# Expert down weights with two neighbouring rows per partition, and the gated rows turned with a stride of two

## The reference, cut to what matters

```python
def hier_moe(h, w_rg, b_rg, w_re, b_re, w_g, w_u, w_d):
    ...
    gates = jnp.sum(jax.nn.one_hot(ids, N_EXPERTS, dtype=jnp.float32) * wts[..., None], axis=1)
    hid = jax.nn.silu(jnp.einsum("nd,edf->nef", x, w_g)) * jnp.einsum("nd,edf->nef", x, w_u)
    y = jnp.einsum("nef,efd->nd", hid * gates[:, :, None].astype(x.dtype), w_d)
```

## Time and profile before

| | us |
|---|---|
| median of 3 runs (842.76 to 843.53) | 843.4 |
| the profiled execution's own time | 847.0 |
| its span in the trace | 845.0 |
| PE busy | 785.5 (93%) |
| DVE busy | 321.5 (38%) |
| ACT busy | 166.5 (20%) |
| moved by DMA | 291.47 MB, mean 345 GB/s |

### The profile page before, as it was taken

One profiled execution on the slowest core, in us unless ns is written; L12 is line 12 of the kernel. 1 busy time (PEld: TensorE's weight loads), 2 busy tenths in 40 slices (PEclk: granted clock), 3 DMA queues, 4 the chain that ended last, 5 costly groups with the idle time before them and its releaser, 6 DMA issues.

```text
span 845.0 us, 15981 instructions
## 1 busy us (share of the span) xinstructions
PE 785.5 (93%) x6910; PEld 524.4 (62%) x6910; DVE 321.5 (38%) x687; ACT 166.5 (20%) x323; POOL 12.3 (1%) x17
## 2 busy tenths in 40 slices
PE   3999999998999999999977989989999999998697
PEld 3788568677898655556542444679865545664244
DVE  1155467653414433433332340223353344333224
ACT  3112411323203111111100141040321111111013
POOL 0000001020000000000000000000000000000000
PEclk9999999999999999999998999999999999999798
DMA  9999779493899599999999999996549999999993
GB/s 342 387 371 386 254 261 353 147 344 104 274 390 399 222 414 363 362 417 415 420 415 411 400 387 385 389 409 243 200 147 417 384 361 417 416 419 415 413 402 144
DMA packets 97879, 291.47 MB, mean 345 GB/s; under 512 B 11833, under 2 KB 14991, under 8 KB 87567
## 3 DMA queue, kind: packets, MB, share of 16 engines
q1 hardware_dynamic: 86960, 284.32, 87.3%
q10 hardware_dynamic: 10847, 6.11, 2.5%
HBM read 288.30 MB, written 2.10 MB: 344 GB/s over the span
## 4 chain that ended last, share of the span: by engine, by line
PE 74%; SPq 11%; DMA 7%; DVE 2%; ACT 2%; issue 2%; ACTq 1%; DVEq 0%
PE psum L1360 7%; PE psum L1262 7%; PE psum L905 7%; PE psum L1335 6%; PE psum L1345 6%; PE psum L1392 5%; PE psum L858 5%; PE psum L965 5%; DMA scratch<-in_w_exp_up 5%; SPq L742 5%; PE psum L1536 4%; PE psum L1549 3%; PE psum L1403 3%; SPq L761 2%; PE psum L1027 2%
## 5 line engine op out<-in xcount | busy, mean ns | idle before, releaser
L1345 PE MATMUL psum<-scratch,hT 128*32 128x512 f32 (+1 forms) x384 | 77.0, 647 | 16.5 <-DMA ring<-in_w_exp_up 8.7
L1335 PE MATMUL psum<-scratch 128*128 128x128 f32 x704 | 82.9, 276 | 0.9 <-DVE scratch L2478 0.9
L1335 PEld LDWEIGHTS psum<-scratch 128*128 128x128 f32 x704 | 80.5, 192 | 1.3 <-issue 1.2
L1345 PE MATMUL psum<-ring,hT 128*32 128x512 f32 (+1 forms) x288 | 67.7, 619 | 5.1 <-DMA scratch<-in_w_exp_up 5.1
L905 PE MATMUL psum<-hT,ring 128*128 128x256 f32 x256 | 57.8, 383 | 1.1 <-DVE hT L2069 0.7
L1403 PEld LDWEIGHTS psum<-const,scratch 128*128 128x128 bf16 x480 | 45.1, 97 | 21.5 <-issue 13.6
L1403 PE MATMUL psum<-const,scratch 128*128 128x256 bf16 x480 | 55.9, 272 | 1.5 <-DVE scratch L2494 1.5
L1345 PEld LDWEIGHTS psum<-scratch,hT 128*32 128x32 f32 (+1 forms) x384 | 21.0, 122 | 54.1 <-issue 54.1
L905 PEld LDWEIGHTS psum<-hT,ring 128*128 128x128 f32 x256 | 47.9, 190 | 9.6 <-DVE hT L2069 2.0
L2487 DVE TENSOR_SCALAR hT<-psum,const 128x512 f32<-128x512 f32 x22 | 16.5, 751 | 95.1 <-PE psum L1392 93.6
L1903 ACT ACTIVATE scratch<-psum 128x256 f32<-128x256 f32 x22 | 8.4, 383 | 211.4 <-PE psum L1345 124.8
(11 more groups left out here) (337 smaller groups left out, 1033.0 us busy)
## 6 DMA issues: line engine op xcount, KB each, us to landing
ring<-in_w_mod SPq DMA_DIRECT2D x40, 1024.0 KB, 11.2
scratch<-in_w_exp_down SPq DMA_DIRECT2D x28, 1024.0 KB, 15.7
ring<-in_w_exp_down SPq DMA_DIRECT2D x24, 1024.0 KB, 17.5
scratch<-in_w_exp_gate SPq DMA_DIRECT2D x22, 1024.0 KB, 16.6
scratch<-in_w_exp_up SPq DMA_DIRECT2D x22, 1024.0 KB, 18.3
ring<-in_w_exp_gate SPq DMA_DIRECT2D x18, 1024.0 KB, 15.5
ring<-in_w_exp_up SPq DMA_DIRECT2D x18, 1024.0 KB, 18.6
scratch<-in_w_exp_gate SPq DMA_DIRECT2D x26, 512.0 KB, 8.0
```

The source lines that it names most:

```text
L1335: last = mm(bank[b][:, k * P:(k + 1) * P], hrow[:, t, half * 4 + k, :], Pm[:, t, :], start=(t == 0), stop=(t == 1))
L1345: last = mm(bank[0][i * m:(i + 1) * m, :], xg[:, k, i * m:(i + 1) * m], w[e][:, k, :, :], start=(k == 0), stop=(k == KT - 1))
```

## The change

The down weights are taken with rows 2p and 2p + 1 in partition p, in all three functions that load them. The two rows are neighbours in HBM and in SBUF, so `expert_down` now moves one piece of 8 KB per partition where there were two of 4 KB. In `half_down` the pieces stay at 2 KB, only the rows change. The single expert of a slot is no longer split by a (128 partitions with 4 KB each, twice) but by partitions: first the partitions 0 to 63, then 64 to 127 (`HB` is 64), with 8 KB each. To match, `turn` transposes the even columns of `hid` for a = 0 and the odd ones for a = 1, read with a stride of two, instead of the first and the second 128.

```diff
             def half_down(l, c, ids, half):
-                wd = I["w_exp_down"][l].rearrange("e (a p) n -> e p a n", a=2)
+                wd = I["w_exp_down"][l].rearrange("e (p a) n -> e p a n", a=2)
...
             def expert_down(l, c, ids):
-                wd = I["w_exp_down"][l].rearrange("e (a p) n -> e p a n", a=2)
+                wd = I["w_exp_down"][l].rearrange("e (p a) n -> e p a n", a=2)
...
                     if len(ids) == 2:
                         sp.dma_start(dst, wd[e]).then_inc(full[s], 16)
                     else:
-                        for a in range(2):
-                            sp.dma_start(dst[:, a], wd[e][:, a]).then_inc(full[s], 16)
+                        for r in (slice(0, HB), slice(HB, P)):
+                            sp.dma_start(dst[r], wd[e][r]).then_inc(full[s], 16)
...
             def turn(sem):
                 for a in range(2):
-                    nc.tensor.transpose(bank[0][:, a * P:(a + 1) * P], hid[:, a * P:(a + 1) * P], ident)
+                    nc.tensor.transpose(bank[0][:, a * P:(a + 1) * P], hid.rearrange("p (n a) -> p a n", a=2)[:, a, :], ident)
```

## The result

The changed kernel takes 863.9 us, median of 5 runs (860.9 to 866.9), against 843.5 us before (842.8 to 844.3). The ratio is 1.0225, with a 95% interval of 1.0194 to 1.0256: 19 us slower by the ratio, 20.3 us by the medians. 850.5 was predicted, with 855.5 as the upper end.

A forecast was written before the change was run, and what follows sets the result against it. The prediction took the full DMA queue late in both expert stages as the bound. Its terms, -2.6 + 9.7 + 0 + 0 = +7.1 us on 843.4, gave 850.5 us, range 840.4 to 855.5.

The forecast's parts named there:

- What bounds the kernel: Late expert stages, both layers: the full DMA queue bounds; its changes reach the end nearly one for one.
- Part 1: Whole down loads, line 761: 8 KB pieces gain 0.065 us for each of 20 experts a layer, 2.6 us in both.
- Part 2: Split down loads, line 764: 64 partitions load at half rate, +2.43 us for each of four experts, +9.7 us.
- Part 3: half_down, line 751: pieces stay 2 KB in the same number, behind the last gate and up loads; zero.
- Part 4: The turn's strided transposes: taken as zero; doubling would add 0.22 us per turn, at most 1.8 us in all.
- Does the cost reach the end?: Last half of pass 10: PE's wait grows to 2.9 and 3.1 us, whole delay kept, no clock loss taken.
- rival 4: Half rate, plus longer waits lowering PE's clock (3.0 us) and strided turns costing double (1.8 us): 855.3 us; chance 0.10.
- Rival 1: Line 764's 64-partition loads run at full rate; all 22 experts a layer gain 0.065 us: 840.5 us; chance 0.19.
- Rival 2: Engines out of step hide half of the split loads' loss, +1.2 us per split expert: 845.7 us; chance 0.12.
- Rival 3: Larger pieces in the down loads gain nothing and the halves cost nothing: 843.4 us; chance 0.09.

The follow-up runs named there:

- the version with no one-sided load: The changed kernel with line 764 alone put back to two loads over all 128 partitions, 4 KB pieces each: 843.2 us, ratio 0.9985.
- the long run: Eight halves following one another in the changed kernel with every whole down load (line 761) split by partitions too; that kernel took 984.8 us, single run.
- the split alone: The kernel before with only line 764 changed to partitions 0 to 63, then 64 to 127, two 4 KB pieces per partition: 867.3 us, ratio 1.0285.

## Why the prediction was wrong

**What bounds the kernel** was read rightly. The loss of the queue reached the end, also that of the mono some 100 us ahead of it, as the run with only the mono's expert split shows. Whether the queue would swallow something at 343 or 684 no run tests: all four holes lie behind these points.

**Part 1**, the larger pieces: -2.6 us predicted. The rate is there (422 GB/s in the window 398:418, and packets as computed), and the five runs without a one-sided load show -1.3, -1.1, -2.4, -1.7 and -3.4 us (the last for partitions 32 to 95), with intervals of about 2 us to either side. All five have the sign, and in two of them the interval leaves out zero. Their mean, 2.0 us, is near the 2.6 to 2.9 that were expected.

**Part 2** is the step that failed, in one term: "+2.43 us, four times, +9.7 us". Which resource and which direction were right; the term's size was wrong, because the price of the ends of a run was not in it, a mechanism that no row of before showed. The term measures 20.2 us, 5.1 for an expert. It has three pieces.
- The half rate itself is 2.16 us for an expert, from the 225 GB/s of the long run. Predicted 2.43.
- The ends of a run of halves slow the whole loads around it. I took the stream as one pipe: a half load at half rate, then full rate again. In the four holes of the changed kernel (rows below) against the run with line 764 put back the loss is 24 x (1 - 339 / 415) = 4.4, 20 x (1 - 327 / 408) = 4.0, 24 x (1 - 366 / 423) = 3.2 and 24 x (1 - 326 / 408) = 4.8 us. The mean is 4.1, so the ends cost 1.9 us there, as against the 2.5 of the long run. This piece was put at nothing.
- 5.1 - 4.1 = 1.0 us for an expert is left, 4 us in all, hardly more than the 3 us to either side of the 20.2.

The four holes of the changed kernel:

```profile
365.00:389.00 24.00, 24.00 (x202) 14.18 (x204) 8.18 (x13) 4.32 (x11) 0.00 (x0) 1.00 1.01 339
451.00:471.00 20.00, 13.28 (x98) 3.61 (x97) 4.92 (x6) 1.28 (x2) 0.00 (x0) 0.83 1.02 327
...
718.00:742.00 24.00, 24.00 (x192) 12.69 (x192) 8.49 (x13) 3.70 (x8) 0.00 (x0) 1.00 1.01 366
800.00:824.00 24.00, 18.16 (x144) 9.55 (x144) 6.76 (x10) 1.73 (x5) 0.00 (x0) 0.86 1.02 326
```

Do the first two pieces alone give the other times? With 2.16 us for an expert and 2.5 us for a run of halves, the changed kernel comes out at 4 x 2.16 + 4 x 2.5 = 18.6 us above the version with no one-sided load (measured 20.2), the mono alone at 9.3 (8.4), the kernel with the whole three split at 8 x 2.16 + 4 x 2.5 = 27.3 (27.1), and all down loads split, 44 experts in 14 runs, at 130 (140). The 2.5 was read from the last of these, the other three were not used for it; they agree within their intervals of about 3 us. Only the split alone, 24 us, lies above it by more than its interval.

For what is left there is one sign in the changed kernel. Near the end of layer 0, while its last gate and up load is on its way (it lands at 494.10) and behind it, two windows of the changed kernel read as the first two lines here; the third is the same place in the kernel with the split alone, whose last product of that kind starts at 486.46:

```profile
490.00:494.00 4.00, 2.79 (x25) 2.23 (x24) 0.00 (x0) 0.00 (x0) 0.00 (x0) 1.00 0.84 300
494.00:498.00 4.00, 3.76 (x33) 1.24 (x34) 0.00 (x0) 0.07 (x1) 0.00 (x0) 1.00 0.85 239
...
482.00:486.00 4.00, 2.82 (x25) 2.25 (x24) 0.00 (x0) 0.00 (x0) 0.00 (x0) 1.00 1.04 397
```

At a DMA share of 0.84 some engines have nothing to move while others still bring the load that PE waits for. With 300 and 239 GB/s, where the split alone has 397 and then 387 (486:490), these 8 us lose about 2.5 us, and that doesn't lie in the four windows above. But the split alone has no such stretch (its share is 1.04 there), so it is no fixed part of the price. It is also one execution against another: the two whose windows are compared took 866.9 and 842.1 us, 24.8 apart and not 20.2. That a load is late because its slowest engine is late, and that engines out of step are also why a single pair of halves disturbs the loads before and after it, is an inference. No run here brings the engines into step, and no row tells them apart, so it stays open.

The Trainium skill states in SBUF — State Buffer, section "Door 1: The DMA port swizzle", that bit 6 of the partition number chooses between the two ports of a cluster, and that 0 to 31 cover the same 8 ports as 0 to 63. These runs agree on both: 32 to 95 has no loss (0.9960), the quarters of 32 lose as much as the halves (1.0216 against 1.0225). Its asymptote of 218 GB/s for eight ports stands against 225 measured in the long run. What its section "Can I just issue two DMAs to hit both halves?" says of two such loads, that they serialize, fits too; the runs show that they cost more than that.

**Part 3** was right as far as can be seen: the split alone, without the new rows in the last pass, loses as much. **Part 4** was nearer to zero than to the doubling: 0.02 us per turn in the one that was read.

**Does the cost reach the end?** The wait before the last half was to grow to 3 us. Instead both halves of the last pass wait. In layer 0 it is 2.53 and 1.45 us, since the queue was later than I had it. The clock, rival 4, did fall at the first of them, in the changed kernel's timeline and in the window behind it:

```profile
484.07 1.07 PE L1360 MATMUL psum<-ring,hT 128*32 128x512 f32 x2 [2.53 <-DMA scratch<-in_w_exp_up]
484.08 1.07 PE L1360 MATMUL psum<-scratch,hT 128*32 128x512 f32 x2
484.89 1.10 PE L1360 MATMUL psum<-ring,hT 128*32 128x512 f32 x2
...
484.00:487.00 3.00, 2.93 (x16) 0.91 (x20) 2.33 (x3) 0.00 (x0) 0.00 (x0) 0.50 1.02 399
```

Four products start 0.82 us after the four before, twice the 0.43 at full clock, for 3 us. It costs nothing there, because PE waits again for the second half, 1.45 us at 494.24.

**The rivals.** Rival 1 (full rate) fell with the split alone. Rival 2 (half of the loss hidden, because the engines are out of step) fell too: more was lost than the half rate, not less. Rival 3 (no gain, no loss) fell with the rates. Rival 4 was right in that more is lost than the half rate, but not by its means.

## What to carry to other kernels

A DMA should have partitions on both sides of partition 64: split a load by what lies within each partition, as line 764 did before, or by even and odd partitions, not into 0 to 63 and 64 to 127. In a full queue one such pair cost about twice what its own half rate says, and the price was handed on to the end through 100 us of full queue. If a semaphore's count is the only reason for a second load, the count can be changed instead: one load of 1 MiB was as fast.

## What the runs showed of the hardware that was not expected

- Two halves of an expert among whole loads cost 4.1 us of the queue's time and 5.1 us at the end, against 2.16 us for an expert within a run of halves.
- The DMA share stays at 1.00 while the rate falls to 186 GB/s. So the share alone doesn't show this loss; GB/s does.
- 64 partitions with a step of two load at full rate (420 GB/s in the window with both loads), and so do partitions 32 to 95 (421 GB/s).
- A transpose of float32 columns with a stride of two has a weight load of 204 ns instead of 140 (medians of 44) and a product of 283 instead of 272, yet PE gives up only 0.02 us for two.
- PE's granted clock was 0.50, the 1.2 GHz level, right after a wait of 2.53 us in the changed kernel. It held through the 2.42 us of the earlier trace rows, and with the split alone it was still 1.00 in the first microsecond after a wait of 3.29 us (476:477) and 0.50 from 478 to 480. So the length of the wait before alone does not decide.
